# Eight weight buffers instead of four in the sample's embedding stage of a fused decode step

## The reference, cut to what matters

```python
h = x + mix
h = h + peer(rmsnorm(h, w["norm_ffn"]), w)
gate = jax.nn.sigmoid((rmsnorm(h, w["norm_ple"]) @ w["w_ple_gate"]).astype(F32)).astype(h.dtype)
return h + gate * (p_i @ w["w_ple_proj"])
```

## Time and profile before

| | |
|---|---|
| three runs | 4254.27 us median (4248.66 to 4264.5) |
| the profiled execution, its own time | 4258.77 us |
| its span in the trace | 4257.0 us |
| busy: PE / DVE / POOL / ACT | 2309.4 / 3283.4 / 2271.0 / 522.7 us |
| DMA over the span | 1574.34 MB, mean 370 GB/s |
| of it: q0 (the gathers) / q1 (SP) | 1265.15 / 298.61 MB |

### The profile page before, as it was taken

One profiled execution on the slowest core, in us unless ns is written; L12 is line 12 of the kernel. 1 busy time (PEld: TensorE's weight loads), 2 busy tenths in 40 slices (PEclk: granted clock), 3 DMA queues, 4 the chain that ended last, 5 costly groups with the idle time before them and its releaser, 6 DMA issues.

```text
span 4257.0 us, 24040 instructions
## 1 busy us (share of the span) xinstructions
PE 2309.4 (54%) x8238; PEld 1380.4 (32%) x8238; DVE 3283.4 (77%) x3700; ACT 522.7 (12%) x1098; POOL 2271.0 (53%) x1213
## 2 busy tenths in 40 slices
PE   8999935523988783649875125971000000018967
PEld 4445612323465231347654112371000000013423
DVE  0130399998567997988879997669999999988873
ACT  2121112222012001211111011010000000021001
POOL 0000156744242355677776675257767887767650
PEclk9999966556988896656766556985555555559988
DMA  8648689988998998999989999999999999999997
GB/s 294 249 163 297 246 347 384 393 348 326 424 418 357 381 399 347 390 395 367 420 348 407 391 412 371 424 416 408 417 368 366 413 382 414 402 403 422 423 411 251
DMA packets 223137, 1574.34 MB, mean 370 GB/s; under 512 B 27123, under 2 KB 29683, under 8 KB 46054
## 3 DMA queue, kind: packets, MB, share of 16 engines
q0 software_dynamic: 172944, 1265.15, 73.2%
q1 hardware_dynamic: 48182, 298.61, 18.2%
q10 hardware_dynamic: 1888, 9.03, 0.5%
HBM read 1532.73 MB, written 39.41 MB: 369 GB/s over the span
## 4 chain that ended last, share of the span: by engine, by line
DVE 40%; PE 33%; DMA 10%; issue 7%; POOL 6%; ACT 2%; SPq 0%; DVEq 0%; ACTq 0%
DVE total L2049 16%; DVE ring L2024 14%; PE bank L877 12%; POOL ring L2609 5%; PE bank L1316 5%; PE bank L1353 4%; DMA ring<-in_peer_v,idx_all 4%; DMA ring<-in_peer_u,idx_all 2%; PE bank L1184 1%; PE bank L956 1%; PE bank L908 1%; PE bank L851 1%; DVE front L1800 1%; PE bank L1158 1%; PE bank L1144 1%
## 5 line engine op out<-in xcount | busy, mean ns | idle before, releaser
L2609 POOL DMA_INDIRECT ring<-in_peer_u,idx_all x576 | 1117.3, 1940 | 743.1 <-DVE dots L2024 325.8
L2049 DVE SCALAR_TENSOR_TENSOR total<-ring,gate_all,total 128x2048 f32<-128x2048 f32 x571 | 1342.2, 2351 | 134.7 <-DMA ring<-in_peer_v,idx_all 113.5
L2609 POOL DMA_INDIRECT ring<-in_peer_v,idx_all x576 | 1090.5, 1893 | 633.1 <-DVE total L2049 278.9
L2024 DVE CUSTOM_DVE_ANT_0 ring<-ring,xrow 128x2048 f32<-128x2048 f32 x576 | 1294.3, 2286 | 136.8 <-DMA ring<-in_peer_u,idx_all 133.2
L877 PE MATMUL bank<-front 128*128 128x490 f32 (+3 forms) x1408 | 616.4, 593 | 45.5 <-ACT front L2173 42.2
L851 PE MATMUL bank<-inv_diag,front 128*128 128x128 f32 (+1 forms) x304 | 61.7, 389 | 1029.4 <-DVE inv_diag L1429 991.4
L851 PEld LDWEIGHTS bank<-inv_diag,front 128*128 128x128 f32 (+1 forms) x304 | 58.9, 298 | 1033.7 <-DVE inv_diag L1429 986.3
L877 PEld LDWEIGHTS bank<-front 128*128 128x128 f32 (+1 forms) x1408 | 240.7, 177 | 412.5 <-issue 409.6
L1316 PE MATMUL bank<-front 128*128 128x128 f32 (+2 forms) x1536 | 257.7, 331 | 2.3 <-ACT front L2377 1.2
L1316 PEld LDWEIGHTS bank<-front 128*128 128x128 f32 x1536 | 242.6, 193 | 20.0 <-issue 4.5
L908 PE MATMUL bank<-front 128*128 128x512 f32 x512 | 221.4, 594 | 4.7 <-DMA front<-const_gate_quarters 3.4
(11 more groups left out here) (332 smaller groups left out, 2970.8 us busy)
## 6 DMA issues: line engine op xcount, KB each, us to landing
front<-in_w_in SPq DMA_DIRECT2D x64, 980.0 KB, 6.8
front<-in_w_out SPq DMA_DIRECT2D x48, 1024.0 KB, 9.1
front<-const_query_in SPq DMA_DIRECT2D x48, 1024.0 KB, 9.0
ring<-const_ahead_in POOLq DMA_DIRECT2D x12, 1960.0 KB, 9.5
front<-const_gate_quarters SPq DMA_DIRECT2D x16, 1024.0 KB, 9.2
front<-in_w_ple_gate SPq DMA_DIRECT2D x16, 1024.0 KB, 5.0
front<-const_uq_halves SPq DMA_DIRECT2D x6, 1536.0 KB, 8.4
ring<-in_peer_u,idx_all POOLq DMA_INDIRECT x576, 12.2
```

Of the source, the lines that this page charges most:

```text
L2024: e.tensor_tensor_reduce(out=ring[:, b, :], in0=ring[:, b, :], in1=xrow[:, t % 2, :], scale=1.0, scalar=0.0, op0=ALU.mult, op1=ALU.add, ac ...
L2049: e.scalar_tensor_tensor(out=total, in0=ring[:, b, :], scalar=c1, in1=total, op0=ALU.mult, op1=ALU.add).then_inc(s("summed"), 1)
L2609: e.indirect_dma_start(out=ring[:, k % RING, :], out_offset=None, in_=a[("peer_u", "peer_v")[side]][0], in_offset=bass.IndirectOffsetOnAxi ...
```

## The change

The sample's 18 slabs (2 of the projection, then 16 of the gate) go through eight buffers instead of four: the four of `W`, then a region behind the sample's `p` rows (buffer 4), one over `XTp` behind the sample's own small `XT_last` (buffer 5), `H[:, 1]` (buffer 6) and `G` (buffer 7). Four idle semaphores count the landings of buffers 4 to 7. SP's order becomes: slabs 0 to 3 at once (as before); the wait for the prompt's last rows; the load of the sample's `p`; the four stores; slabs 4 and 5 with no further wait; a wait until all eight stores of the prompt have landed (`y_out`), since buffers 6 and 7 hold rows that are stored; slabs 6 and 7; from slab 8 on each waits for `slabs_used` to say that the slab eight before it has been read. `pT_ple`, `p_row` and `XT_last` are carved in the size that the sample needs. What PE, ACT and DVE compute, and in which order, stays.

```diff
@@ slab_landed
-            return 16 * (n // SLABS + 1 + (n >= PASSES[f"out{AHEAD}"]) - (n >= PASSES["gate1"]) * QUARTERS * QUARTER_CHUNKS // SLABS)
+            return 16 * (n // SLABS + 1 + (n >= PASSES[f"out{AHEAD}"]))
@@ regions
+LAST_SLABS = 8
-        pT_ple = carve(PLE // P, 2 * P, at=y0 + 2 * D)
-        p_row = carve(2, PLE)
-        sig = [Y, G]
+        pT_ple = carve(PLE // P, NS, at=y0 + 2 * D)
+        p_row = carve(PLE)
+        w_last = [W[:, 0, :], W[:, 1, :], W[:, 2, :], W[:, 3, :], carve(D), carve(D, at=KD * NS), H[:, 1, :], G]
+        XT_last = carve(KD, NS, at=0)
+        sig = Y
+        w_last_landed = [(f"w_landed{i}", 16 * (PASSES["gate0"] + AHEAD_CHUNKS - 2 * AHEAD_RING) // SLABS) for i in range(SLABS)] \
+            + [("state_loaded0", 16 * 2), ("state_loaded1", 16 * 2), ("mla_gains_loaded", 16 * 4), ("sample_w_loaded", 16 * 3)]
@@ SP, sample_embedding_loads
-                def between():
-                    prompt_embedding_stores(1)
-                    e.dma_start(p_row[:NS, 0, :], tile_of(a["p_prompt"][0, 0], a["p_sample"][0], PT)).then_inc(s("p_loaded"), 16)
-
-                slabs("gate1", a["w_ple_gate"][0], extra=a["w_ple_proj"][0], between=between)
+                n0 = PASSES["gate1"]
+                for i in range(KD + PLE // P):
+                    if i == LAST_SLABS - 4:
+                        e.wait_ge(s("embedded"), EMBEDDED[1])
+                        e.dma_start(p_row[:NS, :], tile_of(a["p_prompt"][0, 0], a["p_sample"][0], PT)).then_inc(s("p_loaded"), 16)
+                        prompt_embedding_stores(1)
+                    if i == LAST_SLABS - 2:
+                        e.wait_ge(s("y_out"), 32 * PT)
+                    e.wait_ge(s("slabs_used"), n0 + max(0, i - LAST_SLABS + 1))
+                    w, k = (a["w_ple_proj"][0], i) if i < PLE // P else (a["w_ple_gate"][0], i - PLE // P)
+                    e.dma_start(w_last[i % LAST_SLABS], w[k * P:(k + 1) * P, :]).then_inc(s(w_last_landed[i % LAST_SLABS][0]), 16)
@@ PE, sample_embedding (each wait and operand alike)
+                def landed(i):
+
+                    name, count = w_last_landed[i % LAST_SLABS]
+                    e.wait_ge(s(name), count + 16 * (i // LAST_SLABS + 1))
...
-                    e.wait_ge(s(f"w_landed{n % SLABS}"), slab_landed(n))
+                    landed(n)
...
-                        mm = e.matmul(bank[c][:R, :], XT[:, k, 0:R], W[:, n % SLABS, c * BANK:(c + 1) * BANK], start=(k == 0), stop=False)
+                        mm = e.matmul(bank[c][:R, :], XT_last[:, k, :], w_last[n % LAST_SLABS][:, c * BANK:(c + 1) * BANK], start=(k == 0), stop=False)
```

More of the change, by code:

```diff
@@ L557, in _, with slabs @@
         def _(e):
-            def slabs(name, w, col0=0, ncol=D, extra=None, between=None):
-                for k in range(KD + (PLE // P if extra is not None else 0)):
+            def slabs(name, w, col0=0, ncol=D, between=None):
+                for k in range(KD):
                     n = PASSES[name] + k
@@ L564, in slabs @@
                     if n >= SLABS:
[L565 removed]
+                        e.wait_ge(s("slabs_used"), n - SLABS + 1)
                     if name[:4] == "in0_" and name != "in0_0" and SLABS - MT <= k < SLABS:
                         e.wait_ge(s("nt_transposed"), 4 * (NORMS["x", GROUPS[int(name[4:])][k - SLABS + MT]] + 1))
[L568 to L570 removed]
+                    e.dma_start(W[:, n % SLABS, 0:ncol], w[k * P:(k + 1) * P, col0:col0 + ncol]).then_inc(s(f"w_landed{n % SLABS}"), 16)
             def query_slabs(g, part, between=None):
@@ L920, in sample_embedding @@
             def sample_embedding():
-                R, n0, m0 = NS, PASSES["gate1"], 4 * NORMS["ple", PT]
-                gate0 = n0 + PLE // P
+                R, m0, gate0 = NS, 4 * NORMS["ple", PT], PLE // P
+                def landed(i):
+                    name, count = w_last_landed[i % LAST_SLABS]
+                    e.wait_ge(s(name), count + 16 * (i // LAST_SLABS + 1))
                 e.wait_ge(s("embedded"), EMBEDDED[1])
@@ L926, in sample_embedding @@
                 for k in range(PLE // P):
-                    mm = e.transpose(bank[4][:, k * P:k * P + R], p_row[:R, 0, k * P:(k + 1) * P], ident[:R, :R])
+                    mm = e.transpose(bank[4][:, k * P:k * P + R], p_row[:R, k * P:(k + 1) * P], ident[:R, :R])
                 mm.then_inc(s("pT_ple_psum"), 1)
                 e.wait_ge(s("pT_ple_sb"), T)
-                for n in (n0, n0 + 1):
-                    e.wait_ge(s(f"w_landed{n % SLABS}"), slab_landed(n))
+                for i in range(PLE // P):
+                    landed(i)
                 for c in range(4):
                     for k in range(PLE // P):
-                        mm = e.matmul(bank[4 + c][:R, :], pT_ple[:, k, 0:R], W[:, (n0 + k) % SLABS, c * BANK:(c + 1) * BANK],
+                        mm = e.matmul(bank[4 + c][:R, :], pT_ple[:, k, :], w_last[k][:, c * BANK:(c + 1) * BANK],
                                       start=(k == 0), stop=(k == PLE // P - 1))
@@ L961, in sample_embedding @@
                         if c == 0:
-                            e.wait_ge(s(f"w_landed{n % SLABS}"), slab_landed(n))
-                        mm = e.matmul(bank[c][:R, :], XT[:, k, 0:R], W[:, n % SLABS, c * BANK:(c + 1) * BANK], start=False, stop=(k == KD - 1))
+                            landed(n)
+                        mm = e.matmul(bank[c][:R, :], XT_last[:, k, :], w_last[n % LAST_SLABS][:, c * BANK:(c + 1) * BANK], start=False, stop=(k == KD - 1))
                         if c == 3:
@@ L1958, in sample_embedding @@
                     e.wait_ge(s("sigmoid_ready"), EMBEDDED[1] + c + 1)
-                    link(e.tensor_tensor(sig[0][:NS, cols], sig[0][:NS, cols], bank[4 + c][:NS, :], ALU.mult))
-                    e.tensor_tensor(H[:NS, 0, cols], H[:NS, 0, cols], sig[0][:NS, cols], ALU.add).then_inc(s("embedded"), 1)
+                    link(e.tensor_tensor(sig[:NS, cols], sig[:NS, cols], bank[4 + c][:NS, :], ALU.mult))
+                    e.tensor_tensor(H[:NS, 0, cols], H[:NS, 0, cols], sig[:NS, cols], ALU.add).then_inc(s("embedded"), 1)
             def first_route(g):
@@ L2130, in norm_squares @@
                         turned = bank[q] if (use, t) == ("ple", PT) else norm_bank(n, m)
-                        xt = XT_ahead if use == "x" and t in GROUPS[AHEAD] else XTp if use == "ple" and t < PT else XT
+                        xt = XT_ahead if use == "x" and t in GROUPS[AHEAD] else XTp if use == "ple" and t < PT else XT_last if use == "ple" else XT
                         if use == "ffn":
@@ L2462, in sample_embedding @@
                 e.wait_ge(s("pT_ple_psum"), T)
-                e.copy(pT_ple[:, :, 0:NS], four(bank[4], NS)[:, 0:2]).then_inc(s("pT_ple_sb"), 1)
+                e.copy(pT_ple, four(bank[4], NS)[:, 0:2]).then_inc(s("pT_ple_sb"), 1)
                 yield from norm_squares("ple", [PT], lambda t: None)
@@ L2476, in sample_embedding @@
                         e.wait_ge(s("slabs_used"), PASSES["gate1"] + KD + PLE // P)
-                    e.activation(sig[0][:NS, c * BANK:(c + 1) * BANK], bank[c][:NS, :], ACT.Sigmoid, scale=inv)\
+                    e.activation(sig[:NS, c * BANK:(c + 1) * BANK], bank[c][:NS, :], ACT.Sigmoid, scale=inv)\
                         .then_inc(s("sigmoid_ready"), 1)
```

## The result

| | median | lowest to highest | ratio to before |
|---|---|---|---|
| before, 20 runs | 4254.69 us | 4243.29 to 4264.50 | 1 |
| changed, 20 runs | 4263.50 us | 4253.66 to 4275.76 | 1.0022 (95%: 1.0014 to 1.0029) |

The change makes the kernel slower by 0.22%, some 9 us (6 to 12 us by the interval), where +7.5 us was forecast. The forecast was a median of 4261.8 us in a range of 4248 to 4270, and a difference within 0.5%. The profiled execution of the changed kernel took 4259.96 us, with a span of 4258.2.

A forecast was written before the change was run, and what follows sets the result against it. It took the transfers to bound the last gathers, then PE's fold and gate with a wait for gate slab 15. Cost +11.6 and gain -4.1 gave +7.5 us on 4254.3: 4261.8 us, range 4248 to 4270.

The forecast's parts named there:

- The gain, -4.1 us: At gate slab 15: PE's wait goes, 2.2 us, and the clock's fall behind it, 1.9 us.
- The cost, +11.6 us: Last gathers: six more slabs in SP's queue beside them make the last row land 11.6 us later.
- The half shares: Last gathers: SP's slabs and POOL's gathers each get half of 423 GB/s, so 5.25 MB takes 24.8 us.
- my upper bound of +14.9: Last gathers: the cost if all 6.3 MB of slabs went ahead of them at 423 GB/s.
- that rival: Last gathers: the loads take more than their half, up to all 6.3 MB first; +10.8 in sum, chance 0.13.
- not DVE: End of the gathers: the transfers set it, as DVE waits 10.0 us together for seven late rows.
- The start of the tail: Fold and gate start: PE's clock may rise earlier, -2.2 us, or later, +1.2; taken as 0.
- the loads hide: Last gathers: they lose nothing to the slab loads, only the gain is left, 4250.2 us; chance 0.1.
- The limit of about 358 GB/s for a core: HBM to SBUF: by it 10.5 MB would take 29.3 us and the sum be 4.5 us higher; not adopted.
- PE would keep the low clock through the gate: Gate: after the long rest PE stays at 1.2 GHz, +53 us, near 4315; chance 0.02.
- the change would not do what it says: Gate slabs 12 to 15 come late again, cost without gain, +11.6, 4265.9 us; chance 0.03.
- priced it at nothing as work: Projection: moves up some 16 us into a stretch where PE stands still, at no cost.

The follow-up runs named there:

- e3: Changed kernel with transfers 14 to 17 released as with four buffers, after the slab four before has been read; ratio to before 1.0026.
- e6: Kernel before, four buffers, with `p` ahead of the stores and gate slabs from transfer 2 on held until about the last row's landing; ratio to before 0.9994.
- e1: Changed kernel with transfers 4 to 17 held until the second-last expert row is in the sum; ratio to before 0.9990.
- e2: Changed kernel with `p` and the stores moved ahead of transfer 2 and all gate slabs held until about the last row's landing; ratio to before 0.9976.
- e8: e2 with the prompt's four last stores held too, going out behind transfers 2 to 5; ratio to before 0.9964.
- e5: Changed kernel with transfers 4 and 5 early but 6 to 17 held until about the last gathered row's landing; ratio to before 0.9998.
- e4: Kernel before, four buffers, with only the load of `p` moved ahead of the four stores; ratio to before 1.0014.
- e7: e2 with the residual's transposes first and the projection's products waiting until all but four expert rows are in the sum; ratio to before 0.9968.
- e10: e9 with the hold on the gate slabs released two sums earlier; ratio to before 0.9956.
- e11: e8 and e7 together, stores unsplit; ratio to before 0.9978.
- e9: e7 with the last stores held and split: tiles 1 and 3 behind transfer 3, tiles 0 and 2 behind transfer 7; ratio to before 0.9964.

## Why the prediction was right

**The direction and the size** came out (+8.8 us by the medians, +10.8 by the two traces, +7.5 forecast), through both of its steps: a gain of the forecast size and a cost of the forecast mechanism. The cost was 4.4 us larger than forecast in the traces, which the medians show only in part.

**The gain, -4.1 us.** Line 963 and its wait took 17.9 us and now take 13.75: -4.2. From the fold to the end it is 70.1 us, where 71 was forecast. e3 brings back 2.4 us of wait and 1.9 us of slow clock when it brings back the wait. That the fall of the clock follows such a gap each time is not so, as e6 shows.

**The cost, +11.6 us, was undersized: +16.0 by the trace.** The half shares were right (51.0% and 50.3%), and so were six slabs in the queue and `p`, whose products waited for it until 26.6 us after transfer 0 (forecast 25.3). The term that was too small is the volume against which the half was set, "the gathers still have 4.97 + 0.28 = 5.25 MB to move": at the same distance from transfer 0 the gathers of this execution had 5.87 MB left. With equal shares each MB of gathers more counts twice, so these 5.87 MB take 27.8 us and not 24.8. And SP's queue got all of its 6.34 MB through before the last landing, 0.47 more than the gathers, which is another 1.1 us. That is 4.1 of the 4.4 us. The same from the other end: from transfer 0 to the last landing SP moved 12.65 MB instead of 6.90, 5.75 more; at 423 GB/s that is 13.6 us. The gathers moved 16.09 MB instead of 15.52 in the same stretch, 1.3 us. Those two are 14.9 of the 16.0. The second is no effect of the change that I can show: the two executions stood differently at transfer 0 (the 9th sum began 24.7 us after it before and 26.3 us after it in the changed one; in e1, where both queues had moved the same bytes as there up to then, it began at 24.0). So +16.0 lies a little above my upper bound of +14.9, and all 6.3 MB did go ahead of the last row, though not by the mechanism of that rival: the shares stayed equal up to about 4180, and only then did the gathers' share thin out (33.3%, 23.3% and 21.5% in the next three us).

**A reading that was too simple.** I read from DVE's waits that the transfers set the end of the gathers, "not DVE". But before, the last six sums ran back to back (14.74 us, with a wait of 0.33 us ahead of them): the last row landed just as DVE came free. Transfers and DVE were level there. So a later row counts in full, as it did, but an earlier one gains little; e2 and e8, where eight and then sixteen sums ran back to back, show DVE setting the pace.

**The start of the tail.** I took 0 between -2.2 and +1.2. The gate took 42.45 us for 43.51, -1.1: the clock rose a little earlier, counted from the fold. Over all traces with a resting PE ahead of the fold the gate took 42.45 to 43.96 us (43.51 lies inside), so I can't put the 1.1 us down to the change.

**The rivals.** That the loads hide is refuted by e1 and e5. The limit of about 358 GB/s for a core, which the prediction cites from the Trainium skill (DMA: Bandwidth & Descriptors, Where 436 GB/s comes from) and which would have made the cost larger, does not bind here: the changed kernel moves 427 GB/s of slabs and gathers from 4160 to 4172, and the measurement decides. That PE would keep the low clock through the gate: the grant is 1.00 from 4200 on. That the change would not do what it says: no wait for a slab is left.

**What hid behind what.** The projection moved up by 15 us and cost nothing by itself, but it freed two buffers early; e4 shows that this alone costs 4.3 us at the last landing with four buffers. I had priced it at nothing as work, which was right, and had counted its two transfers in the six.

## What to carry to other kernels

A prefetch is free only where the DMA engines have room. In this kernel the gathers fill them, and each slab of 1.05 MB that was loaded beside them delayed the last gather by about its own transfer time (2.3 to 2.9 us a slab between the traces, 2.5 at 423 GB/s). So the time to ask for the slabs is the landing of the last gather, not the moment at which a buffer comes free. The eight buffers were a loss by themselves (+0.22%) and part of a gain together with a wait that held their loads back (e2, -0.24%). By the traces that wait alone brought 7.1 us (e6) and the buffers 2.7 us on top of it (e2 against e6); the runs don't confirm this split, since e6's own gain lies inside the noise. And when one engine stands still ahead of the tail, move work of its own up to the tail's start, so that it enters with its clock high: worth 3.3 us of the fold in e7, but the work has to reach right up to it, since in e10 PE paused for 2.24 us ahead of the fold, its clock fell, and 3.0 us were lost again.

## What the runs showed of the hardware

- Two queues with rows of 8 KB shared the 16 engines evenly (51.0% and 50.3% from 4160 to 4172 in the changed kernel). The landing of the last gather follows the bytes of both queues, 402 to 411 GB/s from transfer 0 on, with no, two and six slabs behind the stores (e1, e5, changed).
- A gap of PE of 2.2 to 2.4 us was followed by a stretch at 1.2 GHz in three kernels (before, e3, and e4, where it is two gaps of 0.9 and 1.3 us close together) and not in e6. Gaps of 1.1 us (e7), 1.4 us (e11, its first) and 1.5 us (e8) were not followed by one; 0.55 and 1.9 us close together (e9), 2.24 us ahead of the fold (e10) and 5.2 us (e11) were.
- The narrow products (64 columns) of the kernel before, line 941 there, did not hold the clock, though PE counts as busy in them: the grant was 0.52 from 4179 on the earlier trace rows. With the wide products directly ahead of the fold the same 32 records of the fold take 3.79 us instead of 7.09 (e7), all at 1.00, though they are narrow too.
